# Attention-like heads turned to tokens on the partitions, gate blocks as three fp32r products, and two smaller moves in one fused two-layer kernel

## The chip, the cores and the metric

One NeuronCore of one Trainium2 chip runs the whole kernel as one program. The metric is the device time of one execution in microseconds (us), given as the median over executions.

## The reference

Two layers work on 256 tokens of width 1024, all in float32. The first layer mixes four branches and ends in a feed-forward part: a root-mean-square norm, an up projection to 2 x 2816 channels, a causal convolution of three taps, SiLU gating and a down projection. The second layer, with 16 meta tokens ahead of the 256, is where most of the change lies. In outline:

```
h = rmsnorm(x); proj = h @ w_in_2          # u, ml input, z, gates
y_s5 = s5_branch(u)                        # complex scan over time, 32 groups
# mLSTM-like branch, 4 heads of 256
D[t,s]  = exp(cf[t] - mx[t] + ig[s] - cf[s]) for s <= t
W[t,s]  = (q_t . k_s) / 16 * D[t,s]
num[t]  = sum_s W[t,s] v_s
den[t]  = max(|sum_s W[t,s]|, exp(-mx[t]))
head    = num / den * sigmoid(z), normed over its 256 channels, * gain + skip * conv
out     = sigmoid(g_s) * (glu(y_s5) @ w_ssm_out) + sigmoid(g_m) * (heads @ w_ml_out)
x       = x + out @ w_out
```

Behind it comes a product-key expert layer: 128 x 128 experts, 8 heads, the best 16 of each; for each of 128 blocks of experts the kernel makes all activations (`u` blocks), weights them and sums the value blocks.

## The kernel before, in words

The program is written engine by engine with semaphores; the order of work on each engine is the order of the text. Weights are streamed by the SP queue as blocks of 128 x 1024 floats (512 KB) into a ring of eight slots. A product is either plain fp32 (`channels`, line 234: eight matmuls of 256 columns, each of which the trace shows as two passes) or, for accuracy at less time, "three": weight and input are each split into a rounded fp32r high part and an fp32r low part, and high x high, high x low and low x high are added (`three`, lines 263 to 265: 24 matmuls a block). The high part is a copy on ScalarE (`part_high`, line 254), the low part a subtraction on VectorE or GpSimd (`part_low`, line 258, and its kin).

**First feed-forward part** (lines 1296 on). ScalarE squares the eight tiles of x, GpSimd adds four pairs (line 1244), and TensorE sums them over the partitions with four matmuls (line 1309) before the first weight blocks, `up(-4)` and `up(-2)` (lines 1327 to 1329). VectorE turns the sum into a reciprocal (lines 1398, 1399), ScalarE takes the root. The low part of block -4 is VectorE's at line 1145, queued behind its last addition into x.

**z and gates** (lines 1542 to 1556). Twenty-four blocks of `w_in_2` give, channels on partitions, the eight z tiles (g < 8) and two times eight gate tiles (g from 8 to 15, and 16 to 23). `z_products(pe, n)` does the next n of them, placed by hand between other steps of TensorE so as to cover waits; `z_reads` takes them from PSUM on ScalarE. Their ring slots are 0 to 3. Eight are done ahead of the heads, eight within the loop over heads (two each), two behind it, then `outputs(7)`, then six.

**Heads** (TensorE from line 2138, VectorE from 1835, ScalarE from 1957). For each of four heads hh, with the S5 pairs 2hh and 2hh+1 woven in, TensorE's order is: scores (2141, 2145), `inputs(2hh)` (2115, 2117), a z block, the `sel` product that spreads exp(-mx) over the partitions (2155), nine matmuls (2162) for the two halves of the head, channels on partitions, and for the denominator with ones as stationary operand, `outputs(2hh-1)` (2132, 2135), `inputs(2hh+1)`, a z block, the sums of squares over the partitions with ones (2170), `outputs(2hh)` (it begins at 2127, which waits for `finish_y(hh-1)` of VectorE). VectorE's order is: three log tiles (1839 to 1841), `finish_head(hh-1)` (1827, 1831), two weight tiles (1846, 1847), `rotate` (1795 to 1802) and `scan` (1812, 1814) of pair 2hh, the gating of the head (1855), three 256-wide steps on the denominator `rd` (1857 to 1859), `rotate` and `scan` of pair 2hh+1, `finish_y(hh-1)` (1820), then the root's argument and its reciprocal (1866, 1868). GpSimd turns each scanned pair back in five steps (1598 to 1602) and, behind the last pair, scales the tiles of x (1605, 1608). ScalarE takes exponentials, squares, the root of the head (1974), and reads the z blocks.

**Behind the heads**: the glu products (2218), then blocks in three products again.

**Expert activations** (TensorE from 2579). The first `WHOLE` = 52 of 128 `u` blocks are split as whole blocks, low parts on GpSimd; meanwhile VectorE picks the experts. The others go by halves, with the low parts on VectorE (`half_low`, line 2879). TensorE's line 2609 makes the gates of four tokens in eight passes.

## Time and profile before

| | |
|---|---|
| median of 3 runs | 1584.45 us (1583.94 to 1585.49) |
| the profiled execution, its own time | 1585.22 us |
| its span, first to last instruction | 1583.4 us |
| TensorE matmul busy | 1563.0 us, 99% |
| VectorE busy | 1185.1 us, 75% |
| ScalarE busy | 820.7 us, 52% |
| GpSimd busy | 417.0 us, 26% |
| mean granted TensorE clock | 0.997 |
| chain that ended last | PE 69%, DVE 15%, issue 1%, DMA 1% |

In the rows, PE is TensorE's matmul, PEld its weight load, DVE VectorE, ACT ScalarE, POOL GpSimd. A row "arena<-psum L1855" names what an instruction writes and reads and its line. Matmuls are pipelined: the duration of one (0.28 us) is longer than the distance from one to the next, so the cost of a stretch is read from start to start. A stretch in which TensorE is never idle can be shortened only by giving it less to do; where it is idle the row says for how long and which engine released it.

### The profile page before, as it was taken

How to read it: one execution, taken by the hardware profiler on the slowest of the kernel's cores; microseconds unless marked ns; L12 is line 12 of the kernel's file. 1: busy time of each engine (PE TensorE's matmuls, PEld its weight loads, DVE VectorE, ACT ScalarE, POOL GpSimd, SP SyncE). 2: the span in 40 equal slices, each digit the busy share in tenths (PEclk: the TensorE clock that was granted, in tenths of full speed). 3: DMA queues.
4: the chain of work that ended last, by engine and by line, in shares of the span. 5: the costliest groups of instructions: out<-in, count | busy, mean ns of one | idle time of the engine just before them, and what ended most of it. 6: DMA issues, size and time to landing. Idle time of an engine off the chain costs nothing.

```text
span 1583.4 us, 33604 instructions
## 1 busy us (share of the span) xinstructions
PE 1563.0 (99%) x11742; PEld 1440.4 (91%) x11742; DVE 1185.1 (75%) x2300; ACT 820.7 (52%) x1358; POOL 417.0 (26%) x248
## 2 busy tenths in 40 slices
PE   9999999999999999999999999999999999999998
PEld 8999989999999877899999999999999888888886
DVE  7895157998887877345999997778775777777776
ACT  6584345655543732345554444555555555555555
POOL 0604510444420023574789960000000000000000
PEclk9999999999999999999999999999999999999999
DMA  8434353666655221355588885556557777777773
GB/s 316 149 108 125 117 180 115 201 185 186 186 187 174 81 67 43 131 200 174 161 220 233 234 228 167 179 176 176 178 177 223 250 240 232 241 233 236 244 230 133
DMA packets 93101, 289.58 MB, mean 183 GB/s; under 512 B 10336, under 2 KB 27104, under 8 KB 92768
## 3 DMA queue, kind: packets, MB, share of 16 engines
q1 hardware_dynamic: 92880, 288.33, 58.5%
q8 instruction: 53, 0.87, 0.2%
q10 hardware_dynamic: 144, 0.18, 0.0%
q14 instruction: 24, 0.20, 0.0%
HBM read 270.65 MB, written 17.83 MB: 182 GB/s over the span
## 4 chain that ended last, share of the span: by engine, by line
PE 69%; DVE 15%; issue 1%; DMA 1%; ACT 0%; POOL 0%; DVEq 0%; SPq 0%; POOLq 0%
PE psum L2640 7%; PE psum L2639 7%; PE psum L2638 7%; PE psum L263 7%; PE psum L265 7%; PE psum L264 7%; PE psum L234 4%; PE psum L2609 4%; PE psum L1327 2%; PE psum L1329 2%; PE psum L1328 2%; PE psum L1170 2%; PE psum L2218 1%; DVE arena L2824 1%; DVE arena L2836 1%; DVE arena L2440 1%
## 5 line engine op out<-in xcount | busy, mean ns | idle before, releaser
L265 PE MATMUL psum<-arena_parts,ring_parts 128*128 128x256 f32 (+1 forms) x1848 | 519.1, 281 | 0.0
L263 PE MATMUL psum<-arena_parts 128*128 128x256 f32 (+1 forms) x1624 | 465.7, 287 | 3.1 <-DVE ring_parts L2879 2.1
L2879 DVE TENSOR_TENSOR ring_parts<-ring,arena_parts 128x512 fp32r<-128x512 f32 x408 | 276.1, 691 | 151.9 <-ACT arena_parts L2673 91.5
L265 PEld LDWEIGHTS psum<-arena_parts,ring_parts 128*128 128x128 f32 x1848 | 350.4, 190 | 0.0
L263 PEld LDWEIGHTS psum<-arena_parts 128*128 128x128 f32 x1624 | 306.5, 189 | 4.6 <-issue 3.4
L264 PE MATMUL psum<-h_parts,arena_parts 128*128 128x256 f32 x1024 | 286.8, 280 | 0.0
L258 POOL TENSOR_TENSOR ring_parts<-ring,arena_parts 128x1024 fp32r<-128x1024 f32 x81 | 213.4, 2666 | 63.2 <-ACT arena_parts L254 51.0
L2638 PE MATMUL psum<-arena_parts,x_parts 128*128 128x512 f32 x512 | 201.2, 393 | 0.8 <-DVE x_parts L2915 0.8
L2639 PE MATMUL psum<-ring_parts,x_parts 128*128 128x512 f32 x512 | 201.5, 394 | 0.0
L2640 PE MATMUL psum<-arena_parts,x_parts 128*128 128x512 f32 x512 | 201.2, 393 | 0.0
L264 PEld LDWEIGHTS psum<-h_parts,arena_parts 128*128 128x128 f32 x1024 | 194.2, 190 | 0.0
L2673 ACT ACTIVATE arena_parts<-ring 128x512 fp32r<-128x512 f32 x204 | 128.3, 629 | 102.6 <-PE psum L2640 94.6
L2669 ACT ACTIVATE arena_parts<-ring 128x512 fp32r<-128x512 f32 x204 | 128.6, 630 | 66.6 <-PE psum L2640 57.2
L264 PE MATMUL psum<-arena_parts 128*128 128x256 f32 (+1 forms) x568 | 160.2, 282 | 0.0
L2638 PEld LDWEIGHTS psum<-arena_parts,x_parts 128*128 128x128 f32 x512 | 96.0, 187 | 23.7 <-DVE ring_parts L2879 1.0
L2639 PEld LDWEIGHTS psum<-ring_parts,x_parts 128*128 128x128 f32 x512 | 96.1, 188 | 22.3
L2640 PEld LDWEIGHTS psum<-arena_parts,x_parts 128*128 128x128 f32 x512 | 96.3, 188 | 21.4
L1145 DVE TENSOR_TENSOR ring_parts<-ring,arena_parts 128x1024 fp32r<-128x1024 f32 x66 | 95.6, 1457 | 22.6 <-ACT arena_parts L1140 16.9
L264 PEld LDWEIGHTS psum<-arena_parts 128*128 128x128 f32 x568 | 106.9, 188 | 0.2
L254 ACT ACTIVATE arena_parts<-ring 128x1024 fp32r<-128x1024 f32 x75 | 78.0, 1054 | 52.4 <-DMA ring<-stream 52.3
L1327 PE MATMUL psum<-arena_parts 128*128 128x256 f32 x352 | 98.9, 281 | 0.0
L2690 ACT ACTIVATE arena<-psum 128x512 f32 x64 | 38.3, 598 | 116.9 <-PE psum L2609 116.9
(567 smaller groups left out, 3225.3 us busy)
## 6 DMA issues: line engine op xcount, KB each, us to landing
ring<-stream SPq DMA_DIRECT2D x473, 512.0 KB, 3.7
kept<-arena SPq DMA_DIRECT2D x128, 128.0 KB, 3.0
arena<-kept SPq DMA_DIRECT2D x32, 512.0 KB, 4.7
arena<-first SPq DMA_DIRECT2D x1, 2144.0 KB, 17.0
arena<-second SPq DMA_DIRECT2D x1, 1632.0 KB, 6.9
out<-arena SPq DMA_DIRECT2D x4, 256.0 KB, 2.5
x<-x_t SPq DMA_DIRECT2D x2, 256.0 KB, 4.4
x<-x_t SPq DMA_DIRECT2D x1, 512.0 KB, 5.7
```

Source lines behind the costliest of these rows:

```text
L258: ns.tensor_tensor(low[:, s, :], ring[:, s, :], high[:, s, :].bitcast(F32), ALU.subtract)\
L263: nc.tensor.matmul(dst, stationary[0], moving[0], start=first, stop=False)
L264: nc.tensor.matmul(dst, stationary[0], moving[1], start=False, stop=False)
L265: return nc.tensor.matmul(dst, stationary[1], moving[0], start=False, stop=last_one)
L1145: nc.vector.tensor_tensor(low[:, s, :], ring[:, s, :], high[:, s, :].bitcast(F32), ALU.subtract)\
L1327: mm(b, high[:, s, w], h_high[:, k, :], start=k == 0, stop=False)
L2638: mm(b, gate_high[:, q % 4, t], expert_high[:, m % 2, w], start=False, stop=False)
L2639: mm(b, gate_high[:, q % 4, t], low[:, s, w], start=False, stop=False)
L2640: ins = mm(b, gate_low[:, q % 4, t], expert_high[:, m % 2, w], start=False, stop=last_one)
L2669: nc.scalar.activation(expert_high[:, m % 2, halves[0]], ring[:, s, halves[0]], ACT.Copy)\
L2673: nc.scalar.activation(expert_high[:, m % 2, halves[1]], ring[:, s, halves[1]], ACT.Copy)\
L2879: v.tensor_tensor(low[:, s, w], ring[:, s, w], expert_high[:, m % 2, w].bitcast(F32), ALU.subtract)\
```

## The change

Four parts. The four matmuls of the first feed-forward norm's sums move behind the first half of `up(-4)`. The heads are computed with tokens on the partitions: the weights are the stationary operand and v, with a column of ones behind each head's 256 channels, the moving one, so numerator and denominator come from five matmuls of 257 columns; exp(-mx) is brought to the same form once by two small matmuls; the sums of squares become an accumulating output of ScalarE; the root is applied by ScalarE, and four transposes bring each head back to channels on partitions (`turn_head`), one head later. The z blocks (g < 8) are for this made with tokens on the partitions too, 16 matmuls of 128 columns a block. The last eight gate blocks (g from 16) are made as three fp32r products, with the high parts on ScalarE and the low parts on VectorE, whose order at the end of the loop is written out below. `WHOLE` becomes 53. The diff is cut to its changed lines; "..." marks lines left out, and the lines are moved to the left.

```diff
--- before.py
+++ after.py
@@ -1304,10 +1304,6 @@
-    for k in range(4):
-        pe.wait_ge(S("norm_squares"), normed["squares"] + k + 1)
-        ins = mm(bank[7][:, 0:T], ones, squares[:, 4 + k, 0:T], start=k == 0, stop=k == 3)
-    ins.then_inc(S("norm_total"), 1)
@@ -1328,6 +1324,11 @@
+            if n == -4 and part == 0:
+                for k in range(4):
+                    pe.wait_ge(S("norm_squares"), normed["squares"] + k + 1)
+                    ins = mm(bank[7][:, 0:T], ones, squares[:, 4 + k, 0:T], start=k == 0, stop=k == 3)
+                ins.then_inc(S("norm_total"), 1)
@@ -1501,11 +1502,11 @@
-small = r1.take(24, 16)
+small = r1.take(20, 16)
...
-rd, root_h = r1.take(T), r1.take(T)
-hsq = r1.take(2, T)
+hg, hsq = r1.take(2, T), r1.take(2, T)
+den, h_sums, h_root, expc = r1.take(2, 1), r1.take(2, 1), r1.take(2, 1), r1.take(2, 4)
@@ -1518,7 +1519,9 @@
-kc, vc, vt = a8.take(8, TT), a8.take(8, TT), a8.take(3, D)
+kc_at = a8.at
+kc, vc, vt = a8.take(8, TT), a8.take(8, TT), a8.take(3, 4 * (T + 1))
+vt = vt.rearrange("p s (h e) -> p s h e", h=4)
@@ -1526,34 +1529,77 @@
-zsig, gs_g, gm_g = zg[:, 0:8, :], zg[:, 8:16, :], zg[:, 16:24, :]
+zsig = zg[:, 0:8, :].rearrange("p c t -> p (c t)").rearrange("p (a d) -> p a d", a=2)
+gs_g, gm_g = zg[:, 8:16, :], zg[:, 16:24, :]
...
+by_token = psum[:, 4 * 512:6 * 512].rearrange("p (a n) -> p a n", a=2)
...
-head_gated, head_den, squares_den, y_taken, scale_spread, scales_made, h_scaled, y_open = (
+head_gated, head_summed, squares_summed, y_taken, scale_spread, scales_made, h_scaled, y_open = (
...
+def z_tokens(q, w, b, i):
+    for tt in range(2):
+        for k in range(KT):
+            ins = nc.tensor.matmul(b[:, tt * P:(tt + 1) * P], h[:, k, M + tt * P:M + (tt + 1) * P], w[:, k, :],
+                                   start=k == 0, stop=k == KT - 1)
+    return ins
+Z_PARTS, Z_BLOCKS = 16, 24
+z_high_base = split["blocks"] + 12 + split["apart"]
+z_low_base = len(VECTOR_LOWS)
+z_filled = [pe_at.rounds[s] + 4 for s in range(4)]
+z_h_low = Area(arena_parts[25344], kc_at - 25344).take(KT, T)
+z_h_high = Area(arena_parts[25344], kc_at - 25344 + KT * TT).take(KT, T)
+def z_part_high(act, g):
+    part_high(act, rounded, g % 4, z_filled[g % 4] + g // 4)
+def z_part_low(dve, g):
+    s = g % 4
+    dve.wait_ge(S("high"), z_high_base + g - Z_PARTS + 1)
+    nc.vector.tensor_tensor(low[:, s, :], ring[:, s, :], rounded[:, s, :].bitcast(F32), ALU.subtract)\
+        .then_inc(S("vector_gate_low"), 1)
+def z_parts(g):
+    def mats(q, w, b, i):
+        s = g % 4
+        nc.tensor.wait_ge(S("vector_gate_low"), z_low_base + g - Z_PARTS + 1)
+        if g == Z_PARTS:
+            nc.tensor.wait_ge(S("h_parts"), split["h"] + 6)
+        for k in range(KT):
+            c = slice(k * P, (k + 1) * P)
+            ins = three(b[:, 0:T], (rounded[:, s, c], low[:, s, c]), (z_h_high[:, k, :], z_h_low[:, k, :]),
+                        k == 0, k == KT - 1)
+        return ins
+    return mats
...
-        project(pe, [g % 4], [z_bank(g)], 1, channels(T, M))
+        project(pe, [g % 4], [z_bank(g)], 1, z_parts(g) if g >= Z_PARTS else channels(T, M) if g >= 8 else z_tokens)
...
-        evacuate(act, [g % 4], [z_bank(g)], 1, lambda q, b, i: nc.scalar.activation(zg[:, g, :], b[:, 0:T], func))
+        evacuate(act, [g % 4], [z_bank(g)], 1, lambda q, b, i: nc.scalar.activation(
+            zg[:, g, :] if g >= 8 else zsig[:, :, g * P:(g + 1) * P],
+            b[:, 0:T] if g >= 8 else b[:, 0:T].rearrange("p (a n) -> p a n", a=2), func))
...
+        if Z_PARTS <= g + 3 < Z_BLOCKS:
+            z_part_high(act, g + 3)
@@ -1567,7 +1613,7 @@
-k0_zeroed = poo.n + 1
+k0_zeroed = poo.n + 2
@@ -1588,6 +1634,8 @@
+    pool.wait_ge(S("qkv_done"), 8)
+    poo.link(g.memset(vt[:, :, :, T:T + 1], 1.0))
@@ -1785,6 +1833,8 @@
+    dve.wait_ge(S("ml_cols"), 2)
+    vec.tell(v.tensor_copy(expc, bank[5][:, 16:24].rearrange("p (a h) -> p a h", a=2)), S("ml_cols_read"), 2)
@@ -1822,10 +1872,10 @@
-        dve.wait_ge(S("ml_root"), hh + 1)
+        dve.wait_ge(S("ml_sums"), hh + 1)
...
-            done = step(v.scalar_tensor_tensor(h_ml[:, c, :], h_ml[:, c, :], col("ml_norm_g_2", c), root_h,
-                                               ALU.mult, ALU.mult))
+            done = step(v.tensor_scalar(h_ml[:, c, :], bank[4][:, c % 2 * T:(c % 2 + 1) * T],
+                                        col("ml_norm_g_2", c), None, ALU.mult))
@@ -1852,22 +1902,31 @@
-        vec.tell(v.tensor_tensor(h_ml[:, 2 * hh:2 * hh + 2, :], b3(4), zsig[:, 2 * hh:2 * hh + 2, :], ALU.mult),
+        vec.tell(v.tensor_tensor(hg, by_token[:, :, 0:T], zsig[:, :, hh * T:(hh + 1) * T], ALU.mult),
...
-        vec.link(v.tensor_scalar(rd, bank[5][:, 0:T], -1.0, None, ALU.mult))
-        vec.link(v.tensor_tensor(rd, rd, bank[5][:, 0:T], ALU.max))
-        vec.tell(v.tensor_tensor(rd, rd, bank[5][:, T:2 * T], ALU.max), head_den, ONCE + hh + 1)
+        vec.link(v.tensor_scalar(den, by_token[:, :, T:T + 1], -1.0, None, ALU.mult))
+        vec.link(v.tensor_tensor(den, den, by_token[:, :, T:T + 1], ALU.max))
+        vec.link(v.tensor_tensor(den, den, expc[:, :, hh:hh + 1], ALU.max))
+        vec.link(v.scalar_tensor_tensor(den, den, RMS_EPS, den, ALU.mult, ALU.mult))
...
+        dve.wait_ge(squares_summed, ONCE + hh + 1)
+        vec.link(v.scalar_tensor_tensor(h_root, h_sums, 1.0 / T, den, ALU.mult, ALU.add))
+        vec.tell(v.reciprocal(h_root, h_root), S("ml_inverse"), hh + 1)
...
-        dve.wait_ge(squares_den, ONCE + hh + 1)
-        dve.wait_ge(S("ml_sums"), hh + 1)
-        vec.tell(v.scalar_tensor_tensor(root_h, bank[4][:, 0:T], 1.0 / T, rd, ALU.mult, ALU.add),
-                 S("head_read"), hh + 1)
-        vec.tell(v.reciprocal(root_h, root_h), S("ml_inverse"), hh + 1)
+    for half in range(2):
+        ks = slice(4 * half, 4 * half + 4)
+        dve.wait_ge(S("h_rounded"), split["h"] + 4 + half + 1)
+        v.tensor_tensor(z_h_low[:, ks, :], h[:, ks, M:TT], z_h_high[:, ks, :].bitcast(F32), ALU.subtract)\
+            .then_inc(S("h_parts"), 1)
+    z_part_low(dve, 16)
+    z_part_low(dve, 17)
...
+    z_part_low(dve, 18)
...
+    for g in range(19, Z_BLOCKS):
+        z_part_low(dve, g)
@@ -1915,7 +1974,8 @@
-            read_unit(vt[0:n, st, half * 512:(half + 1) * 512], bank[2 + qn["n"] % 4][0:n, :])
+            read_unit(vt[0:n, st, 2 * half:2 * half + 2, 0:T],
+                      bank[2 + qn["n"] % 4][0:n, :].rearrange("p (h e) -> p h e", h=2))
@@ -1965,13 +2025,20 @@
+        if hh == 2:
+            for half in range(2):
+                ks = slice(4 * half, 4 * half + 4)
+                a.activation(z_h_high[:, ks, :], h[:, ks, M:TT], ACT.Copy).then_inc(S("h_rounded"), 1)
...
-        a.activation(hsq, h_ml[:, 2 * hh:2 * hh + 2, :], ACT.Square).then_inc(S("ml_squares"), 1)
-        act.wait_ge(head_den, ONCE + hh + 1)
-        a.activation(rd, rd, ACT.Square, scale=RMS_EPS ** 0.5).then_inc(squares_den, 1)
+        for tt in range(2):
+            ins = a.activation(hsq[:, tt, :], hg[:, tt, :], ACT.Square, accum_out=h_sums[:, tt, :])
+        ins.then_inc(squares_summed, 1)
...
-        a.activation(root_h, root_h, ACT.Sqrt).then_inc(S("ml_root"), 1)
+        sca.link(a.activation(h_root, h_root, ACT.Sqrt))
+        for tt in range(2):
+            ins = a.activation(hg[:, tt, :], hg[:, tt, :], ACT.Copy, scale=h_root[:, tt, :])
+        ins.then_inc(S("ml_root"), 1)
@@ -2102,6 +2169,10 @@
+    for tt in range(2):
+        ins = mm(bank[5][:, 16 + 4 * tt:20 + 4 * tt], rows[0:4, 3, M + tt * P:M + (tt + 1) * P], ident[0:4, 0:4],
+                 start=True, stop=True)
+    ins.then_inc(S("ml_cols"), 1)
@@ -2135,6 +2206,15 @@
+    def turn_head(hh):
+        pe.wait_ge(S("ml_root"), hh + 1)
+        for c in range(2):
+            for tt in range(2):
+                ins = nc.tensor.transpose(bank[4][:, c * T + tt * P:c * T + (tt + 1) * P],
+                                          hg[:, tt, c * P:(c + 1) * P], ident)
+        ins.then_inc(S("ml_sums"), 1)
@@ -2147,36 +2227,35 @@
+        else:
+            turn_head(hh - 1)
...
-        if hh:
-            pe.wait_ge(S("head_read"), hh)
-        mm(bank[5][:, T:2 * T], sel[0:4, hh, :], rows[0:4, 3, M:TT], start=True, stop=True)
+        if hh == 0:
+            pe.wait_ge(S("ml_cols_read"), 2)
+            pe.wait_ge(poo.steps, k0_zeroed)
...
-        wts = ((d[:, 0:T], 1, P, 0), (d[:, T:T + P], 2, P, P), (d[0:M, 384:640], 0, M, 0))
-        for e in range(3):
-            for j, (w, st, n, tlo) in enumerate(wts):
-                lhs = ones[0:n, :] if e == 2 else vt[0:n, st, hh * T + e * P:hh * T + (e + 1) * P]
-                dst = bank[5][:, tlo:T] if e == 2 else bank[4][:, e * T + tlo:(e + 1) * T]
-                ins = mm(dst, lhs, w, start=j == 0, stop=j == 2)
+        by_tile = (((d[0:M, 384:512], 0, M), (d[:, 0:P], 1, P)),
+                   ((d[0:M, 512:640], 0, M), (d[:, P:T], 1, P), (d[:, T:T + P], 2, P)))
+        for tt, wts in enumerate(by_tile):
+            for j, (w, st, n) in enumerate(wts):
+                ins = mm(by_token[:, tt, 0:T + 1], w, vt[0:n, st, hh, :], start=j == 0, stop=j == len(wts) - 1)
...
-        pe.wait_ge(S("ml_squares"), hh + 1)
-        for c in range(2):
-            ins = mm(bank[4][:, 0:T], ones, hsq[:, c, :], start=c == 0, stop=c == 1)
-        ins.then_inc(S("ml_sums"), 1)
...
+    turn_head(3)
...
-split["h"] += 4
+split["apart"] += Z_BLOCKS - Z_PARTS
+split["h"] += 6
@@ -2395,7 +2474,7 @@
-WHOLE, QUADS = 52, T // 4
+WHOLE, QUADS = 53, T // 4
@@ -2526,7 +2605,7 @@
-                pe.wait_ge(S("vector_gate_low"), len(VECTOR_LOWS) + m + 1)
+                pe.wait_ge(S("vector_gate_low"), len(VECTOR_LOWS) + Z_BLOCKS - Z_PARTS + m + 1)
...
```

## Rows read from the trace of the kernel before

**Rows 1.** TensorE's waits: line, what released it, us in total, times, longest
```profile
PE psum L534 <- DVE arena L588: 2.2, 1, 2.2
PE psum L263 <- DVE ring_parts L2879: 2.1, 1, 2.1
PE psum L1309 <- POOL arena L1244: 1.3, 1, 1.3
```

**Rows 2.** Window behind the half blocks' wait: busy by engine, PEclk, DMA share, GB/s
```profile
947.00:948.00 1.00, 1.00 (x7) 1.00 (x6) 1.00 (x3) 0.00 (x0) 0.00 (x0) 0.52 0.84 318
```

**Rows 3.** TensorE's timeline there: start, us, engine, line, operation
```profile
947.04 0.41 PE L265 MATMUL psum<-arena_parts,ring_parts 128*128 128x256 f32 x1
...
950.45 0.29 PE L263 MATMUL psum<-arena_parts 128*128 128x256 f32 x1
```

**Rows 4.** TensorE's timeline at the start of the first feed-forward part
```profile
272.33 1.46 PE L1309 MATMUL psum<-arena,cst 128*128 128x256 f32 x6
...
275.47 0.47 PE L1327 MATMUL psum<-arena_parts 128*128 128x256 f32 x1
```

**Rows 5.** VectorE's timeline there
```profile
273.26 1.22 DVE L1145 TENSOR_TENSOR ring_parts<-ring,arena_parts 128x1024 fp32r<-128x1024 f32 x1
```

**Rows 6.** TensorE's timeline behind the heads
```profile
644.99 7.17 PE L234 MATMUL psum<-h,ring 128*128 128x256 f32 x32
...
653.09 20.99 PE L234 MATMUL psum<-h,ring 128*128 128x256 f32 x96
673.91 7.07 PE L2218 MATMUL psum<-arena,ring 128*128 128x256 f32 x32
680.98 0.36 PE L263 MATMUL psum<-arena_parts 128*128 128x256 f32 x1
...
686.72 7.07 PE L2218 MATMUL psum<-arena,ring 128*128 128x256 f32 x32
```

**Rows 7.** TensorE's timeline, eight passes of 128 columns in the expert part
```profile
954.85 1.16 PE L2609 MATMUL psum<-x 128*128 128x128 f32 x8
955.76 0.36 PE L263 MATMUL psum<-arena_parts 128*128 128x256 f32 x1
```

**Rows 8.** TensorE's timeline of the second head
```profile
580.74 0.69 PE L2141 MATMUL psum<-arena 4*128 4x256 f32 x2
...
588.65 0.69 PE L2155 MATMUL psum<-arena 4*128 4x256 f32 x2
...
593.70 0.63 PE L2132 MATMUL psum<-arena 128*32 128x128 f32 x8
...
595.86 3.72 PE L234 MATMUL psum<-h,ring 128*128 128x256 f32 x16
...
600.73 0.49 PE L2127 MATMUL psum<-arena 128*128 128x128 f32 x2 [0.29 <-DVE arena L1820]
...
602.15 0.69 PE L2141 MATMUL psum<-arena 4*128 4x256 f32 x2
```

**Rows 9.** VectorE's timeline of the second head
```profile
591.50 0.43 DVE L1814 TENSOR_TENSOR arena<-arena 128x258 f32<-128x258 f32 x1
...
596.04 0.44 DVE L1795 TENSOR_TENSOR arena<-psum,arena 128x272 f32<-128x272 f32 x1
...
600.20 0.48 DVE L1820 SCALAR_TENSOR_TENSOR arena<-arena,par,psum 128x256 f32<-128x256 f32 x1
```

**Rows 10.** VectorE's timeline, a small reciprocal ahead of the heads
```profile
535.79 0.25 DVE L1721 RECIPROCAL arena<-arena 128x16 f32<-128x16 f32 x1
```

**Rows 11.** The page's group of ScalarE's block roundings: busy us, mean ns, idle before
```profile
L254 ACT ACTIVATE arena_parts<-ring 128x1024 fp32r<-128x1024 f32 x75 | 78.0, 1054 | 52.4 <-DMA ring<-stream 52.3
```

**Rows 12.** VectorE's timeline while GpSimd works, feed-forward part and last head
```profile
292.85 4.59 DVE L1145 TENSOR_TENSOR ring_parts<-ring,arena_parts 128x1024 fp32r<-128x1024 f32 x3 [0.23 <-DVE arena L1391]
...
647.60 1.81 DVE L1831 SCALAR_TENSOR_TENSOR arena<-arena,par 128x256 f32<-128x256 f32 x2
```

**Rows 13.** GpSimd's timeline, one turning step of the last pair
```profile
643.94 0.74 POOL L1599 TENSOR_TENSOR arena<-arena 128x258 f32<-128x258 f32 x1
```

## The prediction

> **What bounds the kernel now.** I read the page's busy times first, then TensorE's waits, then timelines of the four places that the change touches, then the granted clock. TensorE is busy 99% of the span. Its named waits are few: the longest are 2.2 us at the start, 2.1 us for a vector subtraction in front of the half blocks and 1.3 us for the norm squares [rows 1]. So a saving counts only where TensorE's own queue gets shorter or such a wait goes, and each moved dependence must be checked for a new wait. One more thing can be read: behind the stall of 2.1 us the granted clock of the slice from 947 is 0.52, the lower of its two levels (1.2 and not 2.4 GHz) [rows 2]. From 947.04 to 950.45 TensorE starts 16 products, 0.213 us each [rows 3]; at the usual 0.12 (below) that is 1.5 us lost. That stall cost 3.6 us, not 2.1. A wait of 1.3 us and the first one of 2.2 us cost nothing of that kind.
>
> **(a) Norm sums behind the first block.** Now eight passes and a wait fill 272.33 to 275.47, 3.14 us [rows 4], of which 1.3 us is the wait [rows 1], so 1.8 us is work. The first block cannot simply take their place: its low half is written by VectorE from 273.26 for 1.22 us [rows 5], so it starts at about 274.5. TensorE then idles 2.15 us, runs the block, and pays the 1.8 us behind it: 2.15 + 1.8 - 3.14 = +0.8 us. VectorE gets the total some 3.5 us later, delays its root, the block -1 low half and the first convolution by about as much, and TensorE needs these only two to three blocks (5.6 to 8.5 us) later; I cost this at nothing, and if that cover were too thin by one operation it would be 0.5 us. The new idle time is 2.15 us against the 2.08 that lowered the clock and the 1.3 that did not; by the nearest row I add 1.5. **(a) = +2.3**, from 0 to +2.8.
>
> **(b) Eight token blocks and two tiny products.** A channel block is 16 passes of 256 columns: six blocks take 653.09 to 673.91, 3.47 us each, 0.217 a pass [rows 6]. With tokens as output rows it is 32 passes of 128; eight such passes take 954.85 to 955.76, 0.114 each [rows 7], so 3.64 us. Eight blocks: +1.4. The two products for expc are four short passes, between nothing and 0.114 each: I take +0.2, as they may overlap their neighbours. ScalarE's PSUM reads keep their size, so they cost nothing new. **(b) = +1.6**, from +0.8 to +2.5.
>
> **(c) The four heads.** The second head stands for all: scores to scores is 580.74 to 602.15, 21.41 us [rows 8]. Out go the sel product and nine sums, 588.65 to 593.70, 5.05 us, for five products of 257 columns, ten passes at 0.217, 2.17 us: -2.88. The ones sums of hsq, four passes, go: -0.87. Four transposes of 128 columns come: one pass each, +0.45 (two passes would be 0.9). But L2127 already waits 0.29 us for VectorE's finish_y, and this wait grows. From the end of the inputs (595.86) VectorE needs until 600.68: turning starts at 596.04 and finish_y at 600.20 for 0.48 [rows 8, 9]. Two small operations now stand in that chain before the scan, by a 16-element reciprocal of 0.25 [rows 10] some 0.5 together; TensorE arrives after one z block, 3.5 us, and waits 4.82 + 0.5 - 3.5 = 1.8 us. Period: 21.41 - 2.88 - 0.87 - 0.29 + 0.45 + 1.8 = 19.6, so -1.8 each for three heads. The first head has no such wait: -2.88 - 0.87, some 0.2 given back to GpSimd's turning: -3.6. The 256-wide reciprocal that VectorE loses stood behind finish_y, and helps nobody. VectorE's three 256-wide steps on rd become four small ones, which only lets it reach the turning at the same moment as TensorE's inputs: its scan's last operation ends at 591.93, 11.2 us from the head's start, product and small steps end at 12.85, and the inputs are done at 7.91 + 0.45 + 2.17 + 2.16 = 12.7. ScalarE's root and two scalings are needed by the transposes only after the wait, the outputs and the scores, some 1.8 + 1.4 + 3.1 = 6.3 us behind the z block; the copies of h and the first weight roundings, 1.05 us each [rows 11], fit in there. **(c) = -3.6 - 5.5 = -9.1**, from -11 (small steps free, half of the wait gone) to -4.6 (below).
>
> **(d) Gate blocks as three products.** Before, from the last outputs of the loop to the first glu product is 644.99 to 673.91, 28.9 us. A three-product block is half of 680.98 to 686.72, 2.87 us, 24 products at 0.12 [rows 6]: 0.6 saved each, 4.8 in all. Yet block 16 needs two halves of h's low part and its own low part, all queued on VectorE behind finish_y(2), and only one outputs group (1.4 us) covers them. GpSimd is turning the last pair then. With GpSimd reading SBUF, three such subtractions of 1024 took 4.59 us [rows 12]; alone one takes 1.22 [rows 5]. So TensorE stands 4.6 - 1.4 = 3.2 us, between 2.1 (no contention) and that. Behind block 17 and the transposes, VectorE does finish_head(3), 0.9 for two scalings of 256 and 1.81 for the two skips beside GpSimd [rows 12], before block 18's low part, 1.5: 4.2 us less outputs(7), 1.1, a second stall of 3.1 (2.0 at least). Sum: 3.2 + 5.7 + 0.45 + 1.1 + 3.1 + 17.2 = 30.75, +1.8. Both stalls are longer than the one that lowered the clock: +3.0. The blocks 19 to 23 take 1.5 of VectorE and 1.05 of ScalarE against 2.87, so they keep up, and so does the ring. **(d) = +4.8**, from -0.5 to +6.
>
> The trace shows the pair slowing each other, 1.53 us for 1.22. The Trainium skill, page SBUF — State Buffer, section Who interferes with whom, says that an operation of VectorE with two SBUF inputs and one of GpSimd that reads SBUF shut each other out for a whole instruction. By that rule each subtraction could wait out a whole GpSimd step of the pair, 0.74 us [rows 13], the first stall would be 3 x 1.96 - 1.4 = 4.5 us and the forecast 1581.7. The sum goes by the row.
>
> **(e) One more whole block.** GpSimd is free there, so TensorE has 2.8 us of work where it stood 2.1 us, and VectorE's halves are there when it is done. The wait and the slow clock go: **(e) = -3.6**, at least -2.1. Next in line is the rows' 0.3 us wait, unchanged.
>
> **Sum.** +2.3 + 1.6 - 9.1 + 4.8 - 3.6 = -4.0 us. The profiled execution took 1585.22 (span 1583.4), and the median of the runs is 1584.45, 0.8 below; from the median the forecast is 1580.4.
>
> **Rivals.** (1) The clean case: no new stall lowers the clock and VectorE isn't held up. (a) +0.8, (b) +1.6, (c) -9.1, (d) 2.1 + 2.0 of stall: -0.4, (e) -3.6: -10.7, 1573.7. For it: the 2.2 us wait at the start left the clock alone; against it: the one inside dense work did not. Chance 0.25. (2) The clock also falls in the loop's three waits of 1.8 us, which lie between the 1.3 that was harmless and the 2.1 that was not: +4.5, so +0.5, 1584.9. Chance 0.18. (3) The slower one: the clock stays low twice as long behind each of the six stalls, since the second stall of the tail follows the first within 9 us and the loop stalls come every 20 us. Its price is 3.0 per stall: (a) +3.8, (b) +1.6, (c) -0.1, (d) +7.8, (e) -3.6, +9.5, 1594. It decides once the low stretches pass some 5 us each. Only one stretch of 3.4 us is shown. Chance 0.05. (4) The change doesn't do what it says at (d): if the two stalls are as forecast, eight cheaper blocks end later than eight dear ones. That is inside my forecast, not beside it.
>
> **Numbers.** Forecast case 0.52, spread from -7 to -1 by its bounds, three quarters of it below -3.2. A difference under 0.2%, 3.2 us, can't be told from none here. Faster: 0.39 + 0.25 and little of the rest, 0.65; same 0.30; slower 0.05. The range runs from the clean case to rival 2 with a microsecond to spare, 1573.5 to 1586.
>
> **What would show it.** (a): idle time of 2.2 us before L1327's kin and the sums behind a block. (c): periods of about 19.6, and a wait of 1.8 at L2127's heirs for finish_y. (d): two waits of TensorE on VectorE subtractions around blocks 16 and 18, and clock slices near 0.5 behind them. (e): no wait at the half blocks, clock 1.00 there. It is wrong if the head period is near 17.8 (the wait didn't come) or if blocks 16 to 23 run without a gap.

## The result and the profile after

The changed kernel took **1589.74 us** (median of 20 runs, 1583.20 to 1591.86) against 1584.83 (20 runs, 1582.55 to 1590.39) on the same chip: ratio **1.0028**, 95% interval 1.0019 to 1.0036. By the ratio it is slower by 4.4 us (the medians lie 4.9 apart) where 4.0 us less was forecast, outside the range. The profiled execution took 1590.97 (span 1589.2).

The page: TensorE's busy time went from 1563.0 to 1558.3, 4.7 us less, in a span that is 5.8 us longer.

```profile
span 1589.2 us, 33956 instructions
PE 1558.3 (98%) x11898; PEld 1442.1 (91%) x11898; DVE 1182.3 (74%) x2313; ACT 833.2 (52%) x1383; POOL 430.8 (27%) x250
```

TensorE's waits (waiting line, releaser: total, times, longest), against [rows 1]:

```profile
PE psum L263 <- DVE ring_parts L1571: 5.5, 2, 3.5
PE psum L2198 <- DVE arena L1870: 5.0, 3, 1.7
...
PE psum L1323 <- DVE ring_parts L1145: 2.0, 1, 2.0
```

All six forecast waits are there, five of them at nearly the forecast lengths (norm sums 2.0 for 2.15; loop 1.68, 1.59, 1.70 for 1.8; first of the tail 3.48 for 3.2), the last one shorter (2.00 for 3.1), and the 2.1 us in front of the half blocks is gone. So the places were right. What they cost was not. The head loop, TensorE's timeline (start, duration, line, shapes, count; idle before):

```profile
583.37 2.54 PE L2225 MATMUL psum<-arena 128*16 128x256 f32 x12
591.09 3.02 PE L2243 MATMUL psum<-arena 16*128 16x257 f32 x10
601.61 0.50 PE L2198 MATMUL psum<-arena 128*128 128x128 f32 x2 [1.68 <-DVE arena L1870]
604.04 4.75 PE L2225 MATMUL psum<-arena 128*16 128x256 f32 x12
625.01 0.49 PE L2198 MATMUL psum<-arena 128*128 128x128 f32 x2 [1.59 <-DVE arena L1870]
627.06 4.18 PE L2225 MATMUL psum<-arena 128*16 128x256 f32 x12
646.94 0.49 PE L2198 MATMUL psum<-arena 128*128 128x128 f32 x2 [1.70 <-DVE arena L1870]
```

The same scores take 2.54 us before the first wait, 4.75 and 4.18 behind the first and second. The windows show why (stretch, busy, count, granted clock, DMA share, GB/s): the clock is at its lower level, 1.2 instead of 2.4 GHz, from 603.2 to 610.0 (6.8 us) and from 627.1 to 630.5 (3.4 us), and again at the norm sums and behind both stalls of the tail. At 947, where [rows 2] have 0.52, it is now 1.00.

```profile
276.00:277.00 1.00, 1.00 (x6) 0.50 0.00 0
...
603.00:604.00 1.00, 1.00 (x4) 0.60 0.14 57
609.00:610.00 1.00, 1.00 (x8) 0.50 0.00 0
...
627.00:628.00 1.00, 1.00 (x4) 0.55 0.00 0
...
657.00:658.00 1.00, 1.00 (x7) 0.59 0.00 0
947.00:948.00 1.00, 1.00 (x11) 1.00 0.55 151
```

The tail, TensorE's timeline and then VectorE's, against [rows 6, 12]:

```profile
651.91 0.55 PE L263 MATMUL psum<-arena_parts,rounded 128*128 128x256 f32 x1 [3.48 <-DVE ring_parts L1571]
660.30 0.60 PE L2214 MATMUL psum<-cst,arena 128*128 128x128 f32 x4
663.89 0.36 PE L263 MATMUL psum<-arena_parts,rounded 128*128 128x256 f32 x1 [2.00 <-DVE ring_parts L1571]
...
683.31 1.03 PE L2297 MATMUL psum<-arena,ring 128*128 128x256 f32 x4
```

```profile
646.40 0.48 DVE L1870 SCALAR_TENSOR_TENSOR arena<-arena,par,psum 128x256 f32<-128x256 f32 x1
646.92 3.07 DVE L1921 TENSOR_TENSOR arena_parts<-h,arena_parts 128x1024 fp32r<-128x1024 f32 x2
649.91 3.41 DVE L1571 TENSOR_TENSOR ring_parts<-ring,rounded 128x1024 fp32r<-128x1024 f32 x2
```

VectorE's three subtractions in front of block 16 run from 646.92 to about 651.6, 4.7 us, as [rows 12] had them. From the last outputs of the loop (648.4) to the first glu product it is now 34.9 us, where it was 28.9.

### The profile page after: what moved, and what is told of

It is laid out like the page before. It is cut to its first block, busy times and chain, and to the rows that moved or that the text cites. A ratio compares the mean times of both kernels' runs of the same rounds, so it can differ in the third digit from the quotient of the medians.

```text
span 1589.2 us, 33956 instructions
## 1 busy us (share of the span) xinstructions
PE 1558.3 (98%) x11898; PEld 1442.1 (91%) x11898; DVE 1182.3 (74%) x2313; ACT 833.2 (52%) x1383; POOL 430.8 (27%) x250
## 4 chain that ended last, share of the span: by engine, by line
PE 80%; DVE 4%; DMA 1%; issue 1%; ACT 0%; DVEq 0%; SPq 0%
PE psum L263 11%; PE psum L265 11%; PE psum L264 11%; PE psum L2719 7%; PE psum L2718 7%; PE psum L2717 7%; PE psum L2688 4%; PE psum L1323 2%; PE psum L1325 2%; PE psum L1324 2%; PE psum L1554 2%; PE psum L1170 2%; PE psum L2297 1%; PE psum L234 1%; PE psum L1340 1%; PE psum L1342 1%
## 5 line engine op out<-in xcount | busy, mean ns | idle before, releaser
L265 PE MATMUL psum<-arena_parts,ring_parts 128*128 128x256 f32 (+1 forms) x1912 | 538.2, 281 | 0.0
L265 PEld LDWEIGHTS psum<-arena_parts,ring_parts 128*128 128x128 f32 x1912 | 363.8, 190 | 0.0
L258 POOL TENSOR_TENSOR ring_parts<-ring,arena_parts 128x1024 fp32r<-128x1024 f32 x82 | 217.8, 2687 | 63.4 <-ACT arena_parts L254 50.9
L1145 DVE TENSOR_TENSOR ring_parts<-ring,arena_parts 128x1024 fp32r<-128x1024 f32 x66 | 90.2, 1373 | 26.5 <-ACT arena_parts L1140 20.8
L263 PE MATMUL psum<-arena_parts,rounded 128*128 128x256 f32 x320 | 95.6, 299 | 6.1 <-DVE ring_parts L1571 5.5
```

What stands on the lines that cost most here:

```text
L258: ns.tensor_tensor(low[:, s, :], ring[:, s, :], high[:, s, :].bitcast(F32), ALU.subtract)\
L263: nc.tensor.matmul(dst, stationary[0], moving[0], start=first, stop=False)
L265: return nc.tensor.matmul(dst, stationary[1], moving[0], start=False, stop=last_one)
L1145: nc.vector.tensor_tensor(low[:, s, :], ring[:, s, :], high[:, s, :].bitcast(F32), ALU.subtract)\
```

## Experiments

Every execution comes with its span and its mean granted clock. Below its upper level the clock has only the half, so (1 - clock) x span is the time lost to it, as an upper bound: nothing is lost where the slow stretch runs into a wait, or where it lies behind TensorE's last product. This splits every kernel's mean into a part lost to the clock and a rest. Ratios are against the kernel before on the same chip; the split is over all executions of a kernel, its mean good to about 0.3 to 0.9 us in either part.

| kernel | median us | ratio (95%) | mean us | lost to the clock | rest |
|---|---|---|---|---|---|
| before, beside A | 1585.89 | | 1586.8 | 3.5 | 1583.3 |
| before, beside B | 1586.28 | | 1586.9 | 3.5 | 1583.4 |
| before, beside C | 1587.01 | | 1587.1 | 3.9 | 1583.2 |
| after | 1589.74 | 1.0028 | 1588.9 | 10.5 | 1578.4 |
| fill (A) | 1583.92 | 0.9977 (0.9961 to 0.9993) | 1583.7 | 2.2 | 1581.5 |
| sums_behind (A) | 1588.09 | 1.0017 (1.0001 to 1.0032) | 1588.8 | 4.9 | 1583.9 |
| whole53 (A) | 1583.70 | 0.9987 (0.9973 to 1.0001) | 1583.9 | 2.9 | 1581.0 |
| no_parts (A) | 1583.18 | 0.9983 (0.9971 to 0.9996) | 1583.4 | 5.4 | 1577.9 |
| y_first (B) | 1585.62 | 0.9993 (0.9982 to 1.0005) | 1585.6 | 8.4 | 1577.2 |
| grouped (B) | 1589.73 | 1.0019 (1.0004 to 1.0035) | 1589.7 | 12.7 | 1577.0 |
| parts18 (B) | 1580.47 | 0.9964 (0.9951 to 0.9977) | 1581.4 | 6.0 | 1575.4 |
| best (B) | 1576.89 | 0.9941 (0.9924 to 0.9958) | 1576.9 | 5.8 | 1571.1 |
| fill_loop (C) | 1587.31 | 1.0003 (0.9990 to 1.0016) | 1587.4 | 7.1 | 1580.3 |
| heads_only (C) | 1582.29 | 0.9974 (0.9963 to 0.9986) | 1582.9 | 4.0 | 1579.0 |
| best_fill (C) | 1577.52 | 0.9942 (0.9924 to 0.9959) | 1578.0 | 2.9 | 1575.1 |

A, B and C are three series, each on one chip with its own runs of the kernel before. The changed kernel stands beside a fourth, in which the kernel before had a mean of 1585.2 and no clocks are given; so it is compared with the others by ratios. That mean is 1.6 to 1.9 us lower than in A, B and C: to compare the changed kernel's rest with the others', add about as much to its 1578.4 (an estimate, which takes the lost time of the kernel before to be the same in all four).

Every row's "lost" also holds about 2 us that cost nothing. In the kernel before, TensorE's last product ends at 1576.5, and the clock is low at the end of the span, where TensorE has no work (windows: stretch, busy, count, clock, DMA share, GB/s):

```profile
1575.00:1577.00 2.00, 1.53 (x7) 1.00 0.00 0
1579.00:1583.00 4.00, 0.00 (x0) 0.50 0.71 262
```

That end accounts for 0.9 to 2.9 us in the thirteen profiled executions. All kernels have it, so differences of the column can be read, its height not; in fill's profiled execution there is no other low stretch.

**fill: idle products in the waits.** If the clock is the cost, giving TensorE something to do in its waits must win, although it adds work.

```diff
+for _ in range(8):
+    mm(bank[7][:, 256:384], ident, ones, start=True, stop=True)
 up(-4)
...
+idle(6)                 # the same product, into a free quarter of bank 3
 pe.wait_ge(y_taken, ONCE + c)
...
+idle(14)
 z_products(pe, 2)
 turn_head(3)
 outputs(PAIRS - 1)
+idle(8)
 z_products(pe, 6)
```

> The changed kernel with work added that nobody reads: products of two constants on TensorE, 8 in front of the first feed-forward block, 6 in front of each of the three loop waits for finish_y, 14 in front of block 16 and 8 in front of block 18. At 0.23 us each they fit within the waits of 2.0, 1.6 to 1.7, 3.5 and 2.0 us, so the vector engine's dates stay as they are. Clock theory (the new waits cost little, the low clock behind them costs the rest): all low stretches go, granted clock 0.997 or more, and the time falls by the half of some 23 us of low clock, about 10 us against the changed kernel, to 1578 to 1581. Rival (the waits and the slower products are the loss, the clock is a by-product of idle time that would have been lost anyway): no faster than the changed kernel, 1588 to 1591.

Measured 0.9977, some 8 us under the changed kernel by the ratios (good to 3), 5.8 by the medians; not as far down as 1578 to 1581, but below both kernels. The waits were filled and the lost time fell from 10.5 to 2.2 us, while the rest rose by 3, or by some 1.5 with the allowance for the series. TensorE did strictly more and ended sooner. Of its waits in the loop 1.0 us is left in all, and its windows have no low clock before TensorE's last product:

```profile
PE psum L2206 <- DVE arena L1872: 1.0, 3, 0.3
```

```profile
600.00:625.00 25.00, 24.65 (x174) 1.00 0.19 59
...
650.00:675.00 25.00, 23.75 (x200) 1.00 0.51 173
```

**sums_behind and whole53: parts (a) and (e) alone**, each on the kernel before.

```diff
# sums_behind
-for k in range(4):
-    pe.wait_ge(S("norm_squares"), normed["squares"] + k + 1)
...
+                        if n == -4 and part == 0:
+                            for k in range(4):
...
# whole53
-WHOLE, QUADS = 52, T // 4
+WHOLE, QUADS = 53, T // 4
```

> The kernel before with the norm sums of the first feed-forward part behind its first block and nothing else. By the forecast's step (a): idle time from 272.3 to 274.5 and 1.8 us of sums later, +0.8 us, and +1.5 more if the clock falls as it did in the changed kernel: 1585.6 to 1587.2. Rival (the idle time of 1.3 us goes and nothing comes): 1583.5.

> The kernel before with 53 whole blocks and nothing else. Clock theory: the wait of 2.1 us goes and the 1.5 us of low clock behind it, 3.6 us less than before, about 1581.2, no PEclk slice under 1 near 947 us. Rival: only the wait goes, -2.1 us. Rival two: the wait moves to the selection's rows, 0.

(a) costs +2.2 us by the medians and 2.7 by the ratio, whose interval runs from 0.2 to 5.1 us (+2.3 forecast); the table splits it as I had, +0.6 work and +1.4 clock (0.8 and 1.5). (e) brings -2.2 (-3.6 forecast). Its wait went, 2.3 us of the rest, but only 0.6 of clock on average. The interval of the ratio runs from -4.3 to +0.2 us and the clock's share is good to about 0.9, so the forecast isn't refuted. The stall itself does lower the clock where it can be seen: all four profiled executions that have it (before, sums_behind, heads_only, and parts18 with 1.9 us) show a low stretch behind it. What may have taken the gain back is another wait: in the profiled execution of whole53 it had 2.2 us and a low clock, where it had 0.4 before; how often that happens isn't shown (TensorE's waits, then windows):

```profile
PE psum L2001 <- ACT arena_parts L1889: 2.2, 1, 2.2
```

```profile
450.00:475.00 25.00, 22.48 (x171) 0.93 0.40 139
```

**no_parts: the change without (d)**, blocks 16 to 23 as plain products.

```diff
-Z_PARTS, Z_BLOCKS = 16, 24
+Z_PARTS, Z_BLOCKS = 24, 24
...
-z_part_low(dve, 16)
-z_part_low(dve, 17)
 finish_head(3)
-z_part_low(dve, 18)
 finish_y(3)
-for g in range(19, Z_BLOCKS):
-    z_part_low(dve, g)
```

> The changed kernel with the last eight gate blocks as plain fp32 products again, heads, token blocks, sums and 53 whole blocks as changed. In the two traces the stretch behind the loop takes 34.8 us after and 28.9 before, so it should be 5.9 us less than the changed kernel, some 1584, and half of that if half of its low clock is only passed on. Rival (the three-product blocks save 4.8 us and the waits would stand elsewhere): equal or slower than the changed kernel.

0.9983 against 1.0028: (d) costs 0.0045, 7.1 us, good to 2.4; the median, 1583.18, is near the expected 1584. The lost time falls from 10.5 to 5.4. Its trace also holds the plainest picture of the clock's part. The three waits of the loop are equal, 1.68, 1.68 and 1.70; the period behind the first is 21.87 us (600.10 to 621.97) and behind the second 20.28, and only the first has a low clock (timeline, then windows):

```profile
600.10 0.49 PE L2184 MATMUL psum<-arena 128*128 128x128 f32 x2 [1.68 <-DVE arena L1870]
621.97 0.49 PE L2184 MATMUL psum<-arena 128*128 128x128 f32 x2 [1.68 <-DVE arena L1870]
642.25 0.49 PE L2184 MATMUL psum<-arena 128*128 128x128 f32 x2 [1.70 <-DVE arena L1870]
```

```profile
603.00:606.00 3.00, 3.00 (x10) 0.61 0.00 0
610.00:625.00 15.00, 13.32 (x91) 1.00 0.23 70
```

**heads_only: parts (b) and (c) alone**: no_parts, with the norm sums put back in front and

```diff
-WHOLE, QUADS = 53, T // 4
+WHOLE, QUADS = 52, T // 4
```

> Only the token blocks and the heads of the change: norm sums in front, gate blocks 16 to 23 plain, 52 whole blocks. My prediction's terms (b) and (c) alone: +1.6 - 9.1 = -7.5 against the kernel before, ratio 0.9953. Theory now, from the changed kernel's trace: +1.2 for the token blocks, five products of a head 0.78 us dearer than I took them (-9.1 becomes -6.0), and 0 to 5 us of half clock behind the loop's waits, different in each execution: -4.8 to 0, in the middle -2.4, ratio 0.9985, and a scatter of more than 3 us between executions. Rival (the products are not dearer, only the clock costs): the fastest executions reach -7 or below, ratio 0.9955 or less.

0.9974, 4.7 us by the medians and 4.1 by the ratio: at the lower edge of the theory, and the lost time is that of the kernel before, 0.0 more, good to about 1. So here the three waits cost little or nothing in clock. In the profiled execution the whole loop ran at 1.00, which lets its work be read undisturbed:

```profile
580.45 2.54 PE L2210 MATMUL psum<-arena 128*16 128x256 f32 x12
588.17 3.02 PE L2228 MATMUL psum<-arena 16*128 16x257 f32 x10
591.12 0.63 PE L2188 MATMUL psum<-arena 128*32 128x128 f32 x8
598.68 0.50 PE L2183 MATMUL psum<-arena 128*128 128x128 f32 x2 [1.68 <-DVE arena L1869]
600.73 2.54 PE L2210 MATMUL psum<-arena 128*16 128x256 f32 x12
640.69 7.17 PE L234 MATMUL psum<-h,ring 128*128 128x256 f32 x32
```

From the end of the first head's scores (566.02) to the end of the loop's last outputs (640.69) it takes 74.7 us; before it was 80.4 (564.60 to 644.99, [rows 6] for its end); in the changed kernel 79.4 (568.95 to 648.4), the difference being the clock. That is -5.7, where (c) said -9.1. The period is 20.28 where I had 19.6. The products of one head, 588.17 to 591.12, take **2.95 us and not 2.17**: 0.78 a head, 3.1 in all, and -9.1 + 3.1 = -6.0.

**grouped: why those products are dear.** TensorE's weight loads (PEld) show 0.33 us of idle time at each change between stationary tiles of 16 rows and of 128; the products there start 0.63 us apart instead of 0.43. This edit makes one change less.

```diff
-by_tile = (((d[0:M, 384:512], 0, M), (d[:, 0:P], 1, P)),
+by_tile = (((d[:, 0:P], 1, P), (d[0:M, 384:512], 0, M)),
```

> The changed kernel with the two products of 16 rows next to each other (by_tile's first pair turned). The five products of 257 columns take 2.95 us a head where ten passes of 0.217 make 2.17. In the trace a product in front of which the number of rows changes takes 0.63 us from start to start. Theory: each change between 16 and 128 rows costs some 0.19 us; two of four go, 2.95 becomes 2.57 us, and the whole some 1.5 us less. Rival one (257 columns or the row step of 257 floats are slow as such): 2.95 us, no change. Rival two (the first product of a group on a bank pays): no change.

The weight loads of one head's products, of after and then of grouped:

```profile
591.09 0.29 PEld L2243 LDWEIGHTS psum<-arena 16*128 16x128 f32 x2 [0.33 <-issue]
591.72 0.30 PEld L2243 LDWEIGHTS psum<-arena 128*128 128x128 f32 x2 [0.33 <-issue]
592.35 0.29 PEld L2243 LDWEIGHTS psum<-arena 16*128 16x128 f32 x2 [0.33 <-issue]
592.97 0.73 PEld L2243 LDWEIGHTS psum<-arena 128*128 128x128 f32 x4 [0.33 <-issue]
```

```profile
589.75 0.41 PEld L2243 LDWEIGHTS psum<-arena 128*128 128x128 f32 x2
590.48 0.73 PEld L2243 LDWEIGHTS psum<-arena 16*128 16x128 f32 x4 [0.33 <-issue]
591.54 0.73 PEld L2243 LDWEIGHTS psum<-arena 128*128 128x128 f32 x4 [0.33 <-issue]
```

Two such gaps are gone and the products take 2.65 us, 0.3 less a head (2.57 expected); with the z block ahead of them, whose last pass the first change also delays, it is 6.21 for 6.60. So rows are what makes them dear, and neither the 257 columns nor the first product of a group: the second group's first product has no gap now. But the time doesn't show the expected 1.5 us: TensorE comes sooner to a wait whose end VectorE sets, and the waits grew from 1.68 to 2.07. With them the lost time rose to 12.7, and the kernel stayed where it was.

```profile
PE psum L2198 <- DVE arena L1870: 6.2, 3, 2.1
```

**y_first: a shorter chain to the wait.** VectorE's `scan` and `finish_y` go ahead of the root, TensorE's `inputs(2 * hh + 1)` ahead of `outputs(2 * hh - 1)`.

```diff
-dve.wait_ge(squares_summed, ONCE + hh + 1)
-vec.link(v.scalar_tensor_tensor(h_root, h_sums, 1.0 / T, den, ALU.mult, ALU.add))
-vec.tell(v.reciprocal(h_root, h_root), S("ml_inverse"), hh + 1)
 scan(2 * hh + 1)
 if hh:
     finish_y(hh - 1)
+dve.wait_ge(squares_summed, ONCE + hh + 1)
+vec.link(v.scalar_tensor_tensor(h_root, h_sums, 1.0 / T, den, ALU.mult, ALU.add))
+vec.tell(v.reciprocal(h_root, h_root), S("ml_inverse"), hh + 1)
...
+inputs(2 * hh + 1)
 if hh:
     outputs(2 * hh - 1)
-inputs(2 * hh + 1)
```

> The changed kernel with two orders turned in the loop over heads: VectorE does the scan and finish_y before the head's root argument, and TensorE does inputs(2hh+1) before outputs(2hh-1), so VectorE can begin to turn some 0.6 us sooner. The wait of TensorE for finish_y is 1.6 to 1.7 us three times in the changed kernel. Clock theory: it shrinks to 0.5 to 0.9 us, the loop has no low clock, and besides some 2.5 us of waits up to 5 us of low clock go: 1584 to 1586 where the changed kernel has 1589.7. Rival (waits only): -2.5 us.

The loop's waits went from 5.0 to 3.5 us and the kernel to 0.9993, some 5.5 us under the changed kernel, more than the waits alone could give and in the expected range; its profiled loop has no low clock. But the first stall of the tail grew from 3.5 to 4.3. VectorE's timeline shows why: the two steps of the root now stand between finish_y and the subtractions, which followed it at once in the changed kernel (646.40 and 646.92); here they begin 1.09 us after its start, not 0.52.

```profile
639.93 0.48 DVE L1870 SCALAR_TENSOR_TENSOR arena<-arena,par,psum 128x256 f32<-128x256 f32 x1
640.45 0.34 DVE L1916 SCALAR_TENSOR_TENSOR arena<-arena 128x2 f32<-128x2 f32 x1
640.82 0.17 DVE L1917 RECIPROCAL arena<-arena 128x2 f32<-128x2 f32 x1
641.02 3.31 DVE L1921 TENSOR_TENSOR arena_parts<-h,arena_parts 128x1024 fp32r<-128x1024 f32 x2
```

**parts18: (d) without its first stall.** Blocks 16 and 17 stay plain and cover the subtractions for block 18.

```diff
-Z_PARTS, Z_BLOCKS = 16, 24
+Z_PARTS, Z_BLOCKS = 18, 24
...
-z_part_low(dve, 16)
-z_part_low(dve, 17)
-finish_head(3)
 z_part_low(dve, 18)
+finish_head(3)
 finish_y(3)
```

> The changed kernel with three-product blocks only from block 18 on, so that blocks 16 and 17 as plain fp32 (7 us) stand over VectorE's low parts of h and of block 18, and with block 18's low part in front of finish_head(3). Theory: both waits behind the loop (3.5 and 2.0 us) go and the low clock behind them with them; the stretch behind the loop falls from 34.8 us to 28.9 - 6 x 0.6 + 0.45 = 25.8, the whole by some 9 us against the changed kernel, to about 1581. Rival (VectorE then lags at finish_head(3) and the later blocks wait): the stretch stays above 28.9.

```profile
647.93 7.17 PE L234 MATMUL psum<-h,ring 128*128 128x256 f32 x32
659.86 0.35 PE L263 MATMUL psum<-arena_parts,rounded 128*128 128x256 f32 x1 [0.28 <-DVE ring_parts L1571]
674.90 7.07 PE L2295 MATMUL psum<-arena,ring 128*128 128x256 f32 x32
```

Of 5.5 us of stalls 0.28 is left, and the tail takes 27.0 us (647.93 to 674.90; 25.8 expected) instead of 34.9. 0.9964 against 1.0028: 10 us for two blocks fewer in the cheaper form. Both parts fell, the lost time by 4.5 and the rest by 3.0, or by nearly 5 with the allowance for the series. The trace is of the slowest of its ten executions (1586.58): it has low stretches in the loop, and the stall at the half blocks is back with 1.9 us and a clock of 0.52 at 951, which (e) was to remove.

**fill_loop: the loop's waits alone filled**, this and nothing else of fill.

```diff
+idle(6)
 pe.wait_ge(y_taken, ONCE + c)
```

> The changed kernel with six idle products of 128 columns in front of each of the three waits of the head loop only; the norm sums and the tail stay as they are. The kernel with fillers at all its waits was 5.8 us under the changed kernel. Theory (the clock falls in the loop's three waits, 3.3 to 6.6 us of half clock for two of them in the profiled execution, some 5 us, and the tail and the norm sums hold the rest): the loop shows no slice under 1.00 between 600 and 650 us, the tail keeps its two low stretches, and the time is 2 to 4 us under the changed kernel, 1585.5 to 1587.5. Rival 1 (only the tail's two long stalls cost clock worth speaking of): within 1 us of the changed kernel, 1588.7 to 1590. Rival 2 (the loop holds all of it): 5 us or more under it, at most 1584.5.

1.0003 against 1.0028, 4.0 us: filling the loop's waits took about 3.4 us off the lost time (10.5 to 7.1, good to 1.9), and 1587.31 is in the expected range. But the tail didn't keep its two low stretches of 6.8 and 3.4 us: in the profiled execution only one of 3.4 us is left, and the second stall, of 2.13 us, is harmless there (windows):

```profile
647.00:648.00 1.00, 1.00 (x6) 0.52 0.00 0
651.00:675.00 24.00, 21.19 (x186) 1.00 0.54 176
```

The loop's third wait ends 1.5 us before the tail's first stall begins. So part of what this edit gains may lie behind the loop and not in it; one trace of each kernel can't separate that.

**best and best_fill: what the runs point to.** The changed kernel with the edits of parts18, y_first and grouped, and with

```diff
+for k in range(4):
+    pe.wait_ge(S("norm_squares"), normed["squares"] + k + 1)
...
-                        if n == -4 and part == 0:
-                            for k in range(4):
```

back in front of the first block; best_fill has the `idle(6)` of fill_loop besides.

> All of it together: norm sums where they were, 53 whole blocks, the loop's two orders turned, the 16-row products side by side, three-product blocks from 18 on. By the parts: before 1584.8, 53 blocks -2 to -3.6, token blocks +1.2, loop -9.1 + 3.1 - 1.5 - 2.5 = -10, behind the loop -3.1: about 1568 to 1571, granted clock 0.997 or more. Rival (the parts only pass their gain on to the next wait): above 1575.

> The combined kernel (norm sums in front, gate blocks from 18 on as three products, scan and finish_y ahead of the root, inputs ahead of outputs, the five products grouped by row count, 53 whole blocks), with six idle products in front of each of the loop's three waits. Without them it was 0.9941 of the kernel before, with one low stretch in the loop in its profiled execution. Theory (what is left of the clock's loss in the loop is one stretch of 3 to 6 us of half clock in an average execution): 1.5 to 3 us less, ratio 0.9922 to 0.9932, and no slice under 1.00 between 580 and 650 us. Rival (waits of 1.56 us leave the clock alone nearly always, and the one stretch was chance): within 1 us, ratio 0.9935 to 0.9947.

best is the fastest: **1576.89 us, 0.9941**, 9.4 us under the kernel before. It misses its expected 1568 to 1571 and falls on the rival's side: the loop's waits are still 1.56 us, since the grouped products and the shorter chain gave their gain to the same wait, and a wait of 2.2 us at line 2065 appears as in whole53, with a low clock. Filling the waits takes the lost time from 5.8 to 2.9, but no time: its profiled execution was 3.2 us ahead of best's behind the two blocks that follow the loop (1.5 of that since before the loop, the 2.2 us wait having stayed away, the rest from a low stretch that best has at 641.5) and ended level with it, at 1575.3; a wait of 1.8 us ahead of the value blocks, 0.9 in best, with a low clock behind it, is part of what it gave back. The rival, no gain, holds.

## Why the prediction was wrong

- **(a)** right: +2.2 measured, +2.3 said, work and clock each near their term.
- **(b)** near: from the first token block to the first scores heads_only's queue slips by 1.2 us against before's, +1.6 said.
- **(c)** the first failure, of size. The step "five products of 257 columns, ten passes at 0.217, 2.17 us" is 2.95. The rate came from channel blocks whose stationary tiles all have 128 rows. The price of the change of rows stood in [rows 8]: the nine sums and sel there take 5.05 us, though by columns (fourteen passes of 256 and six of 128) they would be 3.7, and I took that stretch out at its measured price while putting the new one in by columns. With 2.95 the sum gives -6.0; heads_only's trace shows -5.7. (Three heads at -1.79 are also -5.4 and not the -5.5 of the sum.) The wait, its place, its releaser and its length (1.8 said, 1.7 found) were right.
- **The clock** is the larger failure. I charged the changed kernel for (a) and twice for (d), 1.5 us each, gave 1.5 back for (e), and made the loop's three waits a rival: +3.0 net. The mean lost time went from 3.5 (in A and B) to 10.5, +7.0. Of the three assumptions under it two failed and one is in doubt. "Each low stretch is like the one of 3.4 us" ([rows 3]): behind the loop's first wait, and from the end of the tail's first stall on, it lasts 6.8 us. "The loop's 1.7 us lie between harmless and harmful, chance 0.18": each of them is harmful in some executions and not in others. And "removing the half blocks' stall brings 3.6 us" is neither confirmed nor refuted: whole53 gained 2.9 in the means and 2.2 in the medians, with 3.6 inside the interval.
- **(d)** the forecast had the right sign: +7.1, good to 2.4, against +4.8. Its stalls summed to 5.5 us where I had 6.3; the clock took 5.1 us of the split, where I had 3.0. The three subtractions beside GpSimd took 4.7 us, as the row said, and not the 5.9 of a full exclusion; GpSimd's own steps beside them went from 0.74 to 1.59 us.
- **(e)** -2.2 for -3.6, as above; whole53's interval holds both.

By the ratios the parts are +2.7 for (a), -2.1 for (e), -4.1 for (b) and (c) and +7.1 for (d), +3.6 in all; the whole is +4.4, and each of these is good to some 2 us. By the forecast it was -4.0. Of the 8.4 us between, 3.1 are the products, read from the trace, and 4.0 the clock (7.0 less 3.0), from the mean clocks, with the lost time of the kernel before taken from the other series; the last 1.3 is within what the comparisons can tell. The outcome lies between rival 2 (1584.9) and rival 3 (1594), whose mechanisms both occur, each in part of the executions: rival 3's condition, stretches past 5 us, is met twice in the profiled execution.

Rival (4) came true as far as it went: (d) makes cheaper blocks that end later.

**Left open**: why filling the same three waits of 1.7 us gives back about 3.4 us of clock in the changed kernel (fill_loop, good to 1.9) and why they cost about none in heads_only (good to 1). The two differ in what comes before and behind the loop, not in it. The tail's stall right behind the third wait may be part of the answer, as fill_loop's trace suggests; chance between the executions is another part that can't be ruled out. No run separates them.

## What to carry to other kernels

Where TensorE is busy 98% of the time and another engine sets the end of a wait, a cheaper product moves into the wait, and may turn it into one that lowers the clock: order the waiting side first, and only then cut work. Convert blocks to a cheaper form only from the point where their preparation is covered (parts18), since the first two of eight cost more here than the other six gave. Price a short product from the nearest rows with the same mix of shapes, not from the best rate per column, and read the granted clock of many executions before you price a stall.

## What the runs showed of the hardware

- **Waits of 1.6 to 3.5 us inside dense work lower the granted clock, but not always.** In the changed kernel the low stretches lasted 3.4 us (275.5 to 278.9, 627.1 to 630.5, 664.6 to 668.0) or 6.8 us (603.2 to 610.0, 651.0 to 657.8). Three equal waits of one execution gave one low stretch (no_parts). In the thirteen profiled executions, leaving out waits that another stall follows within 5 us: none of seven waits of 1.18 to 1.33 us was followed by one (norm sums in front, y_first), 6 of 14 of the loop's waits of 1.55 to 1.71 us, and 6 of 7 of the 2.04 us in front of the first block. The wait of 2.2 us at the kernel's start never was. The mean granted clock of the changed kernel lay between 0.990 and 0.997 from execution to execution, and its time follows it, 1583.2 at 0.997 and 1591.9 at 0.990. The Trainium skill, page TensorE: Matmul & The Clock Gate, Part 1, says that what watches TensorE's activity runs freely, not in step with the kernel, so that the point of the change varies between runs. This case agrees, in that equal waits differ.
- **Idle products were cheaper than idle time** where the waits had lowered the clock and the products fitted them: fill took 0.0051 of the ratio off, 8 us, with 48 added products of 128 columns (8, three times 6, 14 and 8). Where little was left to win, in best_fill, they brought no time.
- **A change between stationary tiles of 16 and of 128 rows costs about 0.2 us**: in after, four changes made ten passes take 2.95 instead of 2.17 us, and with two changes fewer the z block and the products together took 6.21 instead of 6.60 us.
